# Experts of a hybrid layer: padding rows skipped in gathers and stores, results scattered to token order, plain loads at the end

## The chip, the cores and the metric

One core of a Trainium2 chip runs the whole layer in one launch. The metric is the device time of one execution in microseconds (us), lower is better. Times of several executions are given as their median.

## The reference, cut to what matters

One layer on 1024 tokens of width 1024 in float32: modulated norm, one projection, a recurrent head group and a sparse attention head group, output projection, then a mixture of experts, then a final modulated norm. The change touches the experts, their routing tables and the end.

```python
def hierarchical_moe(h, w_group, b_group, w_expert, b_expert, e_gate, e_up, e_down):
    ...
    expert = (g_sel[:, None] * EXPERTS_PER_GROUP + top_i).reshape(-1)
    token = jnp.repeat(jnp.arange(n_tok), TOP_K_EXPERT)
    ...
    def expert_block(args):
        tok, w, e = args
        xb = xf[tok]
        hid = jax.nn.silu(xb @ e_gate[e]) * (xb @ e_up[e])
        return (hid @ e_down[e]) * w[:, None].astype(xb.dtype)
    ...
    out = jnp.zeros_like(xf).at[row_tok].add(y.reshape(n_rows, D))
```

Ahead of the first lines left out a group of 8 experts is chosen for each token and the best 2 in it; then the pairs are sorted by expert, and each expert's rows are padded to whole blocks. Behind it come x = x + (1 + gate2) * moe and the final modulated norm. There are 32 experts (width 512) and 2048 pairs of a token and an expert. In blocks of 64 rows the reference's routing of its inputs needs 47 blocks: experts 0 to 7 one each, expert 8 two, 9 and 10 one each, then one or two each, never more. The pairs of experts 0 to 10 are 50, 27, 53, 17, 45, 61, 47, 40, 70, 62 and 35, in 12 blocks.

## The kernel before, in words

The program has stages, each with its own semaphores and a barrier at its end: projection, attention and recurrence, routing ("route") and experts ("experts"). Each engine's list of work is written by hand. SP issues plain DMAs on the queue q1; POOL issues DMAs on q0, among them those that are indirect, where a column of row numbers in SBUF says which rows of a DRAM tensor are moved.

**Projection.** POOL writes zeros over the whole of `expert_rows` in DRAM (L457), 34 stores of 128 rows, while TensorE projects.

**Routing.** Every pair gets a place (`dest`): its block and its row in it. VectorE builds one-hot tables of the rows and of the blocks, and multiplies the latter by the token's number (L1723 to L1726). TensorE multiplies the tables (L1782), and VectorE turns the result into the integers `idx_all` (L1728): column b holds the 64 token numbers of block b. Padding rows hold token 0.

**Experts.** A block is 64 rows. There are three slots of weights. SP fills a slot again as soon as it is free: gate and up weights of expert e+3 (L1817, L1818) after the up matmuls of expert e's last block, the down weights (L1821) after its down matmuls. Weights of experts 0 to 2 are loaded during routing. For block b:

- POOL copies the index column (L1882), waits for it and gathers the 64 token rows into one of two buffers (L1885), three blocks ahead; then it waits for the evicted result of its block and stores it (L1893).
- ScalarE takes the gathered rows (L1926), and makes the tanh of the gate (L1935).
- VectorE scales the turned rows (L1957, L1959), gates the hidden rows (L1971, L1976), and evicts the result (L1966). The result `psum["P0"]` has columns 0 to 511 of the 64 rows in partitions 0 to 63 and columns 512 to 1023 in partitions 64 to 127; it goes to `y_sb[j]`, one of two buffers. Before that VectorE waits for the store of block b-2.
- TensorE does gate (L2049), up (L2056), turning (L2062, L2035 for the next block) and down (L2073) matmuls.

The order on POOL around the store, and the pattern that takes the two halves apart:

```python
with pool.Fori(0, full) as i:
    for j in range(2):
        gather(i * 2 + j + 3, 1 - j, i * 2 + j + 2)
        store(i * 2 + j, j)
...
pool.dma_start(y_d[bass.ds(b * BLK, BLK), :].rearrange("r (h n) -> h r n", h=2), y_sb[j]).then_inc(q(f"y_stored{j}"), 16)
```

The store of the last block is issued by SP (L1853). **The end.** When all stores have landed, POOL gathers for each of eight tiles of 128 tokens the first and the second expert's row by `dest` (L1911), 16 indirect DMAs of 512 KB. SP loads the residual rows `x1` (L1856), three tiles at once after the last store, then one for each tile written. TensorE adds the two rows with their weights (L2093, weights as scaled identities of ScalarE, L1940), VectorE adds the residual (L2004), ScalarE squares (L1943), POOL takes the root (L1875), VectorE scales and shifts (L2015, L2016), SP stores the tile (L1865).

Of the kernel before, what the change touches and what calls it, by code (L numbers as in the profile page):

```python
# [20 lines left out]
I32 = mybir.dt.int32  # L21
# [38 lines left out]
ROWS = ALL_BLOCKS * BLK  # L60
# [69 lines left out]
def sparse_attention_moe_layer(nc, x, c, ada_w, ada_b, norm1_g, w_in, shift_mu, w0, w_decay_up, a0, w_aaa_up,  # L130
# [3 lines left out]
    with ExitStack() as ctx:  # L134
# [36 lines left out]
        y_d = dram("expert_rows", (ROWS, D))  # L171
# [36 lines left out]
        idx_all = sb("idx_all", [BLK, ALL_BLOCKS], I32)  # L208
# [28 lines left out]
        with ExitStack() as scope:  # L237
# [135 lines left out]
            def _(pool):  # L373
# [82 lines left out]
                for i in range(ROWS // P):  # L456
                    pool.dma_start(y_d[P * i:P * i + P, :], Z[:, :, :, :].rearrange("p a b c -> p (a b c)")).then_inc(*sig("rows_zero", i, by=16))  # L457
# [18 lines left out]
                pool.wait_ge(*at("rows_zero", ROWS // P - 1))  # L476
# [1022 lines left out]
        with ExitStack() as scope:  # L1499
# [19 lines left out]
            count_i, count_f, token_f = A.take(ALL_BLOCKS).bitcast(I32), A.take(ALL_BLOCKS), A.take(NT)  # L1519
# [86 lines left out]
            def _(dve):  # L1606
# [114 lines left out]
                dve.wait_ge(*at("tokens", 0))  # L1721
# [3 lines left out]
                by_tile = in_block.rearrange("p (t j) b -> p t j b", j=2)  # L1725
                link(dve, dve.tensor_tensor(by_tile, by_tile, token_f.unsqueeze(2).unsqueeze(3).to_broadcast([P, NT, 2, ALL_BLOCKS]), ALU.mult), "in_block", 0)  # L1726
                dve.wait_ge(*at("rows_found", 0))
                link(dve, dve.tensor_copy(idx_all[:, :], psum["W1"][0:BLK, 0:ALL_BLOCKS]), "idx_all", 0)  # L1728
# [57 lines left out]
        with ExitStack() as scope:  # L1786
# [5 lines left out]
            xT, y_sb = A.take(KD, BLK), [A.take(D // 2) for _ in range(2)]  # L1792
            hid, hidT = A.take(DE // 2), A.take(KE // 2, 2, BLK)
            index_now = [A.take(1)[0:BLK].bitcast(I32) for _ in range(2)]
# [4 lines left out]
            first, second, x1 = (A.take(NT, D) for _ in range(3))  # L1799
# [15 lines left out]
            def _(sp):  # L1815
# [35 lines left out]
                full = sp.value_load(first_block[0:1, NE + 2:NE + 3], min_val=NE // 2 - 1, max_val=MAX_BLOCKS // 2)  # L1851
# [3 lines left out]
                def load_x1(t):  # L1855
                    sp.dma_start(x1[:, t, :], x1_d[tile(t), :]).then_inc(*sig(f"x1_loaded{t}", 0, by=16))  # L1856

                sp.wait_ge(q("last_stored"), 16)
                for t in range(3):
                    load_x1(t)  # L1860
                for t in range(NT):
                    if t + 3 < NT:
                        load_x1(t + 3)
                    sp.wait_ge(*at("out", t))
                    sp.dma_start(out[0, tile(t), :], first[:, t, :]).then_inc(*sig("out_stored", t, by=16))  # L1865
# [3 lines left out]
            def _(pool):  # L1869
# [7 lines left out]
                def gather(b, j, before):  # L1877
# [7 lines left out]
                    pool.indirect_dma_start(rows_in[j], None, xn2_d[:, :], bass.IndirectOffsetOnAxis(ap=index_now[j], axis=0)).then_inc(q(f"gathered{j}"), 16)  # L1885
# [15 lines left out]
                gather(pairs * 2 + 2, 0, pairs * 2 + 1)  # L1901
                pool.wait_ge(q("gathered0"), (pairs + 2) * 16)
                pool.wait_ge(q("gathered1"), (pairs + 1) * 16)

                pool.wait_ge(q("y_stored0"), pairs * 16)
                pool.wait_ge(q("y_stored1"), full * 16)
                pool.wait_ge(q("last_stored"), 16)
                pool.sem_inc(q("stores_seen"))
# [212 lines left out]
```

## Time and profile before

| | |
|---|---|
| Median of 3 runs | 1904.99 us (1904.92 to 1906.54) |
| The profiled execution | 1907.29 us, its span 1905.3 us |
| Busy share of the span | PE 86%, DVE 47%, ACT 29%, POOL 20% |
| Mean granted clock of TensorE | 0.939 |
| q0 (DMAs of POOL) | 37200 packets, 54.08 MB, 9.0% of sixteen engines |
| q1 (DMAs of SP) | 121474 packets, 305.99 MB, 45.0% |

PE is the time of the matmuls, PEld that of loading their weights beside them; DVE is VectorE, ACT ScalarE, POOL GpSimd. The granted clock is given as a share of full speed. The span is from the first to the last instruction; the execution's own time is 2 us longer. A wait is put down to what came last. In a timeline a row such as "x32" is a group of equal instructions in a row, with the time from the first to the last. "Landing" is the time from the issue of a DMA until its data are there.

### The profile page before, as it was taken

The page shows a single profiled execution, that of the slowest core. Times are in us where ns is not written, and L with a number is a line of the kernel's source. Part 1 is how long each engine was busy: PE and PEld are TensorE (multiplying, and loading weights), DVE is VectorE, ACT ScalarE, POOL GpSimd, SP SyncE. Part 2 cuts the span into 40 slices and gives each one's busy share as a digit, 9 for nine tenths or more (in the row PEclk, how much of TensorE's full clock was granted, in tenths as well). Part 3 has the DMA queues.
Part 4 walks back from the last instruction along what each step waited for, and adds up shares of the span by engine and source line. Part 5 has one row for each costly group of instructions (what it writes and reads, how often), then busy time and mean ns, then how long its engine had stood idle before and what let it go on. Part 6 is the DMA issues. An engine that isn't in the chain of part 4 may idle for free. (4 is left out here: it accounts for less than half of the span.)

```text
span 1905.3 us, 40477 instructions
## 1 busy us (share of the span) xinstructions
PE 1645.6 (86%) x16070; PEld 1083.5 (57%) x16071; DVE 904.1 (47%) x1996; ACT 559.9 (29%) x1099; POOL 390.2 (20%) x824
## 2 busy tenths in 40 slices
PE   4999999867778889889886997588989999999966
PEld 2644444336667667667663455455556666666642
DVE  4256686257777767767652235221222222222226
ACT  4115886713334334434331111010101111011111
POOL 7601467601101110100100000111111111111113
PEclk9999999978999999999997997698999999999988
DMA  9883434320021011010002655599999999999927
GB/s 323 269 334 145 161 120 163 119 83 27 14 93 38 13 38 27 13 38 7 19 7 92 250 177 219 189 360 379 381 368 339 316 358 362 362 359 339 305 90 301
DMA packets 158802, 361.83 MB, mean 190 GB/s; under 512 B 33698, under 2 KB 71634, under 8 KB 158674
## 3 DMA queue, kind: packets, MB, share of 16 engines
q1 hardware_dynamic: 121474, 305.99, 45.0%
q0 software_dynamic: 37200, 54.08, 9.0%
q8 instruction: 87, 1.43, 0.3%
q14 instruction: 41, 0.34, 0.1%
HBM read 303.23 MB, written 56.65 MB: 189 GB/s over the span
## 5 line engine op out<-in xcount | busy, mean ns | idle before, releaser
L2049 PE MATMUL psX<-arena 128*64 128x256 f32 x1536 | 188.2, 401 | 28.1 <-DMA arena<-in_e_down_dram 26.6
L2049 PEld LDWEIGHTS psX<-arena 128*64 128x64 f32 x1536 | 119.4, 145 | 109.9 <-issue 63.0
L2073 PE MATMUL psP<-arena 128*64 128x512 f32 x768 | 175.4, 598 | 0.0
L809 PE MATMUL psX<-arena 128*128 128x512 f32 x320 | 142.6, 601 | 3.4 <-DVE arena L715 1.9
L509 ACT ACTIVATE arena<-arena 128x1024 bf16<-128x1024 f32 (+5 forms) x138 | 134.2, 973 | 32.5 <-POOL arena L466 28.6
L809 PE MATMUL psP<-arena 128*128 128x512 f32 x320 | 141.1, 595 | 2.9 <-DVE arena L715 2.9
L1893 POOL DMA_DIRECT2D expert_rows<-arena x47 | 40.9, 869 | 483.5 <-DVE arena L1966 453.3
L1740 PE MATMUL psP<-arena 128*128 128x512 f32 x256 | 117.9, 620 | 9.8 <-DVE arena L1673 4.6
L1926 ACT ACTIVATE arena<-arena 64x1024 f32<-64x1024 f32 x49 | 51.7, 1056 | 238.1 <-PE psT L2035 211.1
L1935 ACT ACTIVATE arena<-psX 128x256 f32<-128x256 f32 x48 | 18.4, 383 | 339.8 <-PE psX L2049 339.8
L1971 DVE SCALAR_TENSOR_TENSOR arena<-arena,psX 128x256 f32<-128x256 f32 x48 | 20.2, 421 | 191.4 <-ACT arena L1935 191.4
L1264 PE MATMUL psP<-ckvT,arena 128*128 128x512 f32 (+3 forms) x192 | 81.5, 537 | 33.7 <-DVE st L1103 22.5
L809 PEld LDWEIGHTS psX<-arena 128*128 128x128 f32 x320 | 60.5, 192 | 79.5 <-issue 74.0
L809 PEld LDWEIGHTS psP<-arena 128*128 128x128 f32 x320 | 59.9, 190 | 79.7 <-issue 75.4
L2073 PEld LDWEIGHTS psP<-arena 128*64 128x64 f32 x768 | 50.9, 136 | 88.0 <-issue 82.2
L2056 PE MATMUL psX<-arena 128*64 128x128 f32 x1536 | 92.1, 273 | 0.0
L2056 PE MATMUL psT<-arena 128*64 128x128 f32 x1536 | 92.1, 273 | 0.0
L1740 PEld LDWEIGHTS psP<-arena 128*128 128x128 f32 x256 | 50.1, 199 | 73.6 <-issue 72.6
L2056 PEld LDWEIGHTS psX<-arena 128*64 128x64 f32 x1536 | 87.4, 137 | 6.7
L1420 PE MATMUL psW<-arena 64*64 64x64 f32 x2304 | 78.8, 225 | 14.2 <-DVE arena L1208 14.2
L1420 PEld LDWEIGHTS psW<-arena 64*64 64x64 f32 x2304 | 73.7, 140 | 24.5 <-DVE arena L1208 18.7
L2056 PEld LDWEIGHTS psT<-arena 128*64 128x64 f32 x1536 | 85.6, 137 | 0.0
(407 smaller groups left out, 2805.3 us busy)
## 6 DMA issues: line engine op xcount, KB each, us to landing
arena<-in_e_gate_dram SPq DMA_DIRECT2D x32, 2048.0 KB, 20.1
arena<-in_e_up_dram SPq DMA_DIRECT2D x32, 2048.0 KB, 25.9
arena<-in_e_down_dram SPq DMA_DIRECT2D x32, 2048.0 KB, 27.2
arena<-in_ada_w_dram SPq DMA_DIRECT2D x12, 2048.0 KB, 14.2
expert_rows<-Z POOLq DMA_DIRECT2D x34, 512.0 KB, 16.5
expert_rows<-arena POOLq DMA_DIRECT2D x47, 256.0 KB, 14.9
proj_T<-arena SPq DMA_DIRECT2D x36, 256.0 KB, 2.0
arena<-in_x_dram SPq DMA_DIRECT2D x16, 512.0 KB, 5.7
```

The lines of the kernel that those rows point to most:

```text
L509: link(act, act.activation(junk_bf[:, 0:n], score[k][:, 0:n], ACT.Sign, scale=s_sgn[k], bias=s_neg[k], accum_out=s_sum[k]), "counted", k, i)
L809: mm = pe.matmul(psum[b], w[:, k, first:first + P], hT[:, k, 512 * half:512 * half + 512], start=(k == 0), stop=(k == KD - 1))
L1264: mm = pe.matmul(psum[f"P{half}"][:, 0:m], qlT[:, 4 * (h % 2) + h // 2, :], ckvT[:, 512 * half:512 * half + m], start=True, stop=True)
L1420: mm = pe.matmul(o, (old, new)[w], (new, old)[w], start=True, stop=True)
L1740: mm = pe.matmul(psum[f"P{half}"], kt(mixT, t)[:, k, :], wout[:, k, 512 * half:512 * half + 512], start=(k == 0), stop=(k == KD - 1))
L1893: pool.dma_start(y_d[bass.ds(b * BLK, BLK), :].rearrange("r (h n) -> h r n", h=2), y_sb[j]).then_inc(q(f"y_stored{j}"), 16)
L1926: act.activation(rows, rows_in[j], ACT.Copy).then_inc(q("rows_ready"), 1)
L1935: act.activation(hid, psum["X0"][:, 0:DE // 2], ACT.Tanh, scale=0.5).then_inc(q("tanh_done"), 1)
L1971: dve.scalar_tensor_tensor(out=hid, in0=hid, scalar=1.0, in1=psum["X0"][:, 0:DE // 2], op0=ALU.add, op1=ALU.mult).then_inc(q("half_gated"), 1)
L2049: mm = pe.matmul(psum["X0"][BLK * h:BLK * h + BLK, 0:DE // 2], xT[:, k, :], gate_w[u][:, k, DE // 2 * h:DE // 2 * (h + 1)], start=(k == 0) ...
L2056: mm = pe.matmul(psum[("X1", "T1")[f]][BLK * h:BLK * h + BLK, 0:P], xT[:, k, :], up_w[u][:, k, at_col:at_col + P], start=(k == 0), stop=(k ...
L2073: mm = pe.matmul(psum["P0"][BLK * half:BLK * half + BLK, :], hidT[:, f, h, :], down_w[u][:, KE // 2 * h + f, D // 2 * half:D // 2 * (half ...
```

## The change

Numbers of pairs, 2 x token + j, take the place of token numbers: `expert_rows` has 2048 rows, two for each token, in token order. Padding rows get the number 4096. From the table `pair_all` come the token numbers (`idx_all`, half of it: 2048 for padding, outside of the 1024 rows). Gathers and stores are indirect with a bounds check, and rows out of bounds are left out. In blocks 0 and 1 padding is clamped to row 1023, so that both buffers hold numbers. The result is evicted in two halves so that each of 64 partitions holds a whole row, and POOL scatters it. The second buffer of results is `Z`. The zeros of the projection stage are gone. At the end SP loads the residual rows once expert 29 is done (in slot 2, which is then free), and after the last scatter the pairs of rows of each tile with one plain load of 1 MB.

```diff
-ROWS = ALL_BLOCKS * BLK
+NO_PAIR = 4 * SEQ
...
-        y_d = dram("expert_rows", (ROWS, D))
+        y_d = dram("expert_rows", (2 * SEQ, D))
...
-                for i in range(ROWS // P):
-                    pool.dma_start(y_d[P * i:P * i + P, :], Z[:, :, :, :].rearrange("p a b c -> p (a b c)")).then_inc(*sig("rows_zero", i, by=16))
...
+                for j in range(2):
+                    link(pool, pool.tensor_scalar(pair_f[:, :, j], token_f, 2.0, float(j - NO_PAIR), ALU.mult, ALU.add), "pairs", j)
...
-                link(dve, dve.tensor_copy(idx_all[:, :], psum["W1"][0:BLK, 0:ALL_BLOCKS]), "idx_all", 0)
+                step(dve.tensor_scalar(pair_all[:, :], psum["W1"][0:BLK, 0:ALL_BLOCKS], float(NO_PAIR), None, ALU.add))
+                step(dve.tensor_scalar(idx_all[:, :], pair_all[:, :], 1, None, ALU.logical_shift_right))
+                link(dve, dve.tensor_scalar(idx_all[:, 0:2], idx_all[:, 0:2], SEQ - 1, None, ALU.min), "idx_all", 0)
...
-                sp.wait_ge(q("y_ready"), pairs * 2 + 1)
-                sp.dma_start(y_d[bass.ds((full * 2 + 1) * BLK, BLK), :].rearrange("r (h n) -> h r n", h=2), y_sb[1]).then_inc(q("last_stored"), 16)
...
+                sp.wait_ge(q("y_done"), two_left + 1)
+                for t in range(NT):
                     sp.dma_start(x1[:, t, :], x1_d[tile(t), :]).then_inc(*sig(f"x1_loaded{t}", 0, by=16))
...
+                for j in range(2):
+                    sp.wait_ge(q(f"y_stored{j}"), pairs * 16)
+                for t in range(NT):
+                    sp.dma_start(both[:, t], y_d[2 * P * t:2 * P * t + 2 * P, :].rearrange("(p j) n -> p j n", j=2)).then_inc(*sig(f"y_loaded{t}", 0, by=16))
...
-                    pool.indirect_dma_start(rows_in[j], None, xn2_d[:, :], bass.IndirectOffsetOnAxis(ap=index_now[j], axis=0)).then_inc(q(f"gathered{j}"), 16)
+                    pool.indirect_dma_start(rows_in[j], None, xn2_d[:, :], bass.IndirectOffsetOnAxis(ap=index_now[j], axis=0),
+                                            bounds_check=SEQ - 1, oob_is_err=False).then_inc(q(f"gathered{j}"), 16)
...
-                    pool.dma_start(y_d[bass.ds(b * BLK, BLK), :].rearrange("r (h n) -> h r n", h=2), y_sb[j]).then_inc(q(f"y_stored{j}"), 16)
+                    pool.sem_inc(q("y_seen"))
+                    pool.tensor_copy(place_now[j], pair_all[:, bass.ds(b, 1)]).then_inc(q("place_ready"), 1)
+                    pool.wait_ge(q("place_ready"), b + 1)
+                    pool.sem_inc(q("place_seen"))
+                    pool.indirect_dma_start(y_d[:, :], bass.IndirectOffsetOnAxis(ap=place_now[j], axis=0), y_sb[j], None,
+                                            bounds_check=2 * SEQ - 1, oob_is_err=False).then_inc(q(f"y_stored{j}"), 16)
...
-                    dve.tensor_tensor(y_sb[j], psum["P0"], gate_half, ALU.mult).then_inc(q("y_ready"), 1)
+                    dve.tensor_tensor(y_sb[j][:, 0:D // 2], psum["P0"][0:BLK], gate_half[0:BLK], ALU.mult).then_inc(q("y_half"), 1)
+                    dve.wait_ge(q("y_half"), b + 1)
+                    dve.tensor_tensor(y_sb[j][:, D // 2:D], psum["P0"][BLK:P], gate_half[BLK:P], ALU.mult).then_inc(q("y_ready"), 1)
```

POOL's list of work at the end of the loop over blocks and after it, before (a name such as `expert_rows<-arena 2x64x512` is destination, source and shape; 48 blocks, the last without a store on POOL):

```order
L1893 DMA expert_rows<-arena 2x64x512
L1882 ISA
L1882 COPY arena<-idx_all 64x1
L1883 REGISTER_ALU
L1885 DMA arena<-xn_rows,arena 64x1024
L1902 ISA
L1903 ISA
L1905 REGISTER_ALU
L1906 REGISTER_ALU
L1911 DMA arena<-expert_rows,dest 128x1024 x10
```

and now:

```order
L1894 DMA expert_rows<-arena 2048x1024
L1878 ISA
L1878 COPY arena<-idx_all 64x1
L1879 REGISTER_ALU
L1881 DMA arena<-xn_rows,arena 64x1024
L1889 REGISTER_ALU
L1891 ISA
L1891 COPY arena<-pair_all 64x1
L1894 DMA expert_rows<-Z,arena 2048x1024
L1905 ISA
L1906 ISA
L1871 TENSOR_TENSOR st<-st,mhalf 128x1 x8
```

The gathers at the end have left POOL, the last store has come to it, and each store has a copy of its row numbers ahead.

SP's list of work after the last weights, before:

```order
L1853 DMA expert_rows<-arena 2x64x512
L1856 DMA arena<-x_rows 128x1024 x4
L1865 DMA out_dram<-arena 128x1024
L1856 DMA arena<-x_rows 128x1024
L1865 DMA out_dram<-arena 128x1024
```

and now:

```order
L1852 REGISTER_ALU
L1854 DMA arena<-x_rows 128x1024 x8
L1856 REGISTER_ALU
L1858 DMA arena<-expert_rows 128x2048 x8
L1861 DMA out_dram<-arena 128x1024 x8
```

All loads of residual rows stand ahead of the wait for the stores, and the result's loads follow it.

## Rows read from the trace of the kernel before

**Rows 1.** Busy time: length, PE, PEld, DVE, ACT, POOL, clock, DMA share, GB/s.
```profile
1216.00:1415.00 199.00, 173.24 (x1588) 115.96 (x1590) 45.46 (x103) 18.70 (x26) 25.01 (x37) 0.92 0.99 356
1415.00:1841.00 426.00, 425.20 (x4270) 288.36 (x4266) 124.00 (x280) 49.32 (x69) 70.08 (x105) 1.00 0.94 322
```

**Rows 2.** Waits of TensorE, 1206 to 1842 us: total, times, longest.
```profile
PE psX L2049 <- DMA arena<-in_e_down_dram: 26.6, 7, 7.6
```

**Rows 3.** Timeline of TensorE, gate matmuls: start, length, engine, line, [idle before <-releaser].
```profile
1215.90 5.98 PE L2049 MATMUL psX<-arena 128*64 128x256 f32 x32 [1.51 <-DVE arena L1959]
...
1270.88 5.36 PE L2049 MATMUL psX<-arena 128*64 128x256 f32 x32 [3.87 <-DMA arena<-in_e_down_dram]
...
1414.81 3.62 PE L2049 MATMUL psX<-arena 128*64 128x256 f32 x32
```

**Rows 4.** Chain that ended last, 1236 to 1410 us: start, length, what.
```profile
1242.76 27.78 DMA arena<-in_e_down_dram
...
1368.49 31.55 DMA arena<-in_e_down_dram
```

**Rows 5.** DMA, 1206 to 1242 us, in 40 slices.
```profile
GB/s 405 423 414 405 164 196 59 189 335 223 350 378 182 96 232 41 0 0 0 0 0 0 14 114 337 396 400 423 405 419 405 419 428 373 406 379 383 388 401 383
```

**Rows 6.** DMA, 1842 to 1851 us: busy tenths and GB/s in 40 slices.
```profile
DMA  0000000111111201101111111111111111100000
GB/s 0 0 0 0 0 0 0 36 18 18 46 27 55 18 0 55 18 27 46 46 46 46 55 55 46 55 46 55 55 46 55 46 55 55 46 0 0 0 0 0
```

**Rows 7.** Timeline in the middle of the experts; landings of L1885 (gather) and L1893 (store).
```profile
1512.32 0.69 DVE L1966 TENSOR_TENSOR arena<-psP,ckvT 128x512 f32<-128x512 f32 x1 [2.07 <-PE psP L2073]
...
1514.55 0.20 POOL L1882 COPY arena<-idx_all 64x1 int32 x1
...
1515.57 0.93 POOL L1885 DMA_INDIRECT arena<-xn_rows,arena  x1 [0.81 <-POOL arena L1882]
...
1516.10 0.42 DVE L1971 SCALAR_TENSOR_TENSOR arena<-arena,psX 128x256 f32<-128x256 f32 x1 [3.09 <-ACT arena L1935]
...
1520.52 1.06 ACT L1926 ACTIVATE arena<-arena 64x1024 f32<-64x1024 f32 x1 [4.46 <-PE psT L2035]
...
1524.47 0.69 DVE L1966 TENSOR_TENSOR arena<-psP,ckvT 128x512 f32<-128x512 f32 x1 [2.07 <-PE psP L2073]
...
DMA to landing us min/median/max: 4.3/15.2/16.2
...
DMA to landing us min/median/max: 9.2/14.9/15.8
```

**Rows 8.** Timeline and chain of the tail; landing of L1856 (residual rows, plain load).
```profile
1841.40 0.69 DVE L1966 TENSOR_TENSOR arena<-psP,ckvT 128x512 f32<-128x512 f32 x1 [2.07 <-PE psP L2073]
...
1842.30 7.94 DMA expert_rows<-arena
...
1851.05 7.68 DMA arena<-expert_rows,dest
...
1858.87 5.38 PE L2093 MATMUL psP<-arena 128*128 128x512 f32 x8 [17.61 <-DMA arena<-expert_rows,dest]
...
1871.81 1.22 DVE L2004 TENSOR_TENSOR arena<-psX,arena 128x1024 f32<-128x1024 f32 x1
...
1879.94 1.23 DVE L2004 TENSOR_TENSOR arena<-psP,arena 128x1024 f32<-128x1024 f32 x1
...
1886.00 1.23 DVE L2004 TENSOR_TENSOR arena<-psT,arena 128x1024 f32<-128x1024 f32 x1 [2.08 <-DMA arena<-x_rows]
...
DMA to landing us min/median/max: 3.2/7.5/9.8
```

**Rows 9.** Timeline of VectorE, end of routing.
```profile
1193.70 0.18 DVE L1718 TENSOR_SCALAR arena<-dest 128x16 int32<-128x16 int32 x1
...
1202.25 0.22 DVE L1728 CAST idx_all<-psW 64x68 int32<-64x68 f32 x1 [4.05 <-PE psW L1782]
```

**Rows 10.** Busy time, 80 to 140 us (columns as in rows 1).
```profile
80.00:140.00 60.00, 57.90 (x215) 25.99 (x214) 32.61 (x79) 9.73 (x19) 18.76 (x35) 1.00 0.85 332
```

More of the change, by code:

```diff
@@ L1720, in _ @@
                 step(dve.tensor_copy(place_f[1], place_i[1]))
-                dve.wait_ge(*at("tokens", 0))
+                dve.wait_ge(*at("pairs", 1))
                 dve.wait_ge(*at("out_done", NT - 1))
@@ L1791, in sparse_attention_moe_layer @@
             rows_in, rows = [piece[0:BLK] for piece in pieces], pieces[0][BLK:P]
-            xT, y_sb = A.take(KD, BLK), [A.take(D // 2) for _ in range(2)]
+            xT, y_sb = A.take(KD, BLK), [A.take(D)[0:BLK], Z[0:BLK].rearrange("p a b c -> p (a b c)")]
             hid, hidT = A.take(DE // 2), A.take(KE // 2, 2, BLK)
-            index_now = [A.take(1)[0:BLK].bitcast(I32) for _ in range(2)]
+            index_now, place_now = ([A.take(1)[0:BLK].bitcast(I32) for _ in range(2)] for _ in range(2))
             assert A.at <= WEIGHTS_AT
@@ L1798, in sparse_attention_moe_layer @@
             A.at = 0
-            first, second, x1 = (A.take(NT, D) for _ in range(3))
+            both, x1 = A.take(NT, 2, D), A.take(NT, D)
             assert A.at == (SLOTS - 1) * (2 * KD * DE + KE * D)
@@ L1901, in _ @@
                 gather(pairs * 2 + 2, 0, pairs * 2 + 1)
+                store(full * 2 + 1, 1)
                 pool.wait_ge(q("gathered0"), (pairs + 2) * 16)
                 pool.wait_ge(q("gathered1"), (pairs + 1) * 16)
[L1905 to L1908, printed above, removed]
                 for t in range(NT):
-                    for j, dst in enumerate((first, second)):
-                        pool.indirect_dma_start(dst[:, t, :], None, y_d[:, :], bass.IndirectOffsetOnAxis(ap=dest[:, t, j:j + 1], axis=0))\
-                            .then_inc(*sig(f"gathered{j}{t}", 0, by=16))
-                    if t >= 4:
-                        roots(t - 4)
-                for t in range(NT - 4, NT):
                     roots(t)
@@ L2014, in write @@
                         dve.wait_ge(*at("rows_loaded", 3))
-                    step(dve.scalar_tensor_tensor(out=first[:, t, :], in0=res[:, b, :], scalar=s_x[:, 16 + t:17 + t], in1=gain_row, op0=ALU.mult, op1=ALU.mult))
-                    link(dve, dve.tensor_tensor(first[:, t, :], first[:, t, :], shift_row, ALU.add), "out", t)
+                    step(dve.scalar_tensor_tensor(out=both[:, t, 0, :], in0=res[:, b, :], scalar=s_x[:, 16 + t:17 + t], in1=gain_row, op0=ALU.mult, op1=ALU.mult))
+                    link(dve, dve.tensor_tensor(both[:, t, 0, :], both[:, t, 0, :], shift_row, ALU.add), "out", t)
                 add(0)
@@ L2087, in _ @@
                         pe.wait_ge(*at("x2", t - 4))
-                    for j, rows_of in enumerate((first, second)):
+                    pe.wait_ge(*at(f"y_loaded{t}", 0))
+                    for j in range(2):
                         pe.wait_ge(*at("weights", t, j))
-                        pe.wait_ge(*at(f"gathered{j}{t}", 0))
                         for half in range(2):
                             part = slice(512 * half, 512 * half + 512)
-                            mm = pe.matmul(psum["PTXW"[t % 4] + str(half)], weigh[:, t, j, :], rows_of[:, t, part], start=(j == 0), stop=(j == 1))
+                            mm = pe.matmul(psum["PTXW"[t % 4] + str(half)], weigh[:, t, j, :], both[:, t, j, part], start=(j == 0), stop=(j == 1))
                     mm.then_inc(*sig("combined", t))
```

18 lines of the change are left out of this document (5 added, 13 removed).

## The prediction

> **What bounds the kernel now.** I read the page's engine shares, then busy time by stretch, then the waits of TensorE, then single timelines. The experts take the last third. From 1216 to 1415 us TensorE is busy 173 of 199 us at a mean granted clock of 0.92; from 1415 to 1841 it is busy 425 of 426 us at 1.00 [rows 1]. So the first stretch can be shortened from outside and the second cannot. The waits of TensorE name the landing of the down weights, 26.6 us over seven times [rows 2]. After a wait the gate matmuls also run long: 5.36 us for 32 instead of 3.62 [rows 3]. Undisturbed, one block follows another after 12.15 us (1512.32 to 1524.47, two evictions in [rows 7]). The first block starts at 1215.90 and the fourteenth at 1414.81 [rows 3]; thirteen blocks at 12.15 are 157.9 us, so 41.0 us are lost. The first block's slow start is 2.4 of it (5.98 against 3.62). **38.6 us** hang on the weights, and a single 0.8 us wait later on.
>
> The weights come in 2.097 MB transfers. Where they flow freely, in seven slices in a row, the sixteen DMA engines move 400 to 428 GB/s [rows 5], about 412, or 5.1 us a transfer. The down weights of expert 4 land at 1270.5 and those of expert 11 at 1400.0 [rows 4]: 129.5 us for 21 transfers, which alone need 107.1. The other 22.4 us fall on the eight blocks computed between them, **2.8 us for each pair** of a gather and a store. By their bytes (0.524 MB) they should cost 1.27. The remaining 1.53 us is the shape of the store, I think. The last store of the kernel runs with nothing beside it, and it moves at 46 to 55 GB/s, with the engines busy at one tenth [rows 6]: two engines out of sixteen. Its shape is halves, rows, columns, 2x64x512, like all the other stores. Weights striped over all engines must wait for the two that are late.
>
> The tail is a serial chain: eviction to 1842.1, store to 1850.2, gather to 1858.7, the first combining matmuls (5.4 us), then VectorE at 4.07 us a tile to the end (1871.81 to 1879.94 are two), with one wait of 2.08 us for residual rows [rows 8].
>
> **The change, part by part.**
>
> *Zero stores (34 of 512 KB) removed.* They lie in 80 to 140 us, where TensorE is busy 57.9 of 60 us [rows 10], and nothing there waits for a DMA. At most the 2.1 us of idle time comes back; I take 0. Their cover is the projection's matmuls.
>
> *Two tables instead of one.* The conversion of 0.22 us becomes one of the same size plus two integer operations on the path to the first gather, of some 0.18 us as their neighbour [rows 9]: **+0.4 us**. The two POOL operations that number the pairs stand far ahead of a wait.
>
> *Eviction in two halves.* 64x512 twice instead of 128x512 once: 0.69 us again if time goes by the columns, 0 if by bytes; I take 0.7. In the loop this is free: VectorE's next work is 3.8 us after the eviction's start (1512.32 to 1516.10, [rows 7]) and the two halves end after 1.4.
>
> *Scatter instead of store.* POOL gains a copy and the wait for it, 1.02 us by the gather's (1514.55 to 1515.57, [rows 7]). Queued behind it is the next gather. It is now issued 0.7 + 1.0 us later. Today it is issued at 1515.57 and lands 15.2 us later, at 1530.8. ScalarE takes a block's rows every 12.15 us; the row at 1520.52 is the block before, so these rows are taken at 1532.7. The slack of 1.9 us shrinks to 0.2, and the rows so taken are turned by TensorE only some ten microseconds later (in its next block). Free.
>
> *Less and better spread traffic.* The reference's routing gives 47 blocks and an empty one. The first twelve blocks hold 507 pairs in 768 rows. The stores move 507 rows, the gathers 558, since the first two blocks clamp their padding to a real row. That is 0.69 of the bytes, 0.88 us a pair of transfers. With 64 rows as the leading dimension the scatter has the shape of the gather. For the cost of its shape the bounds are 0 and the 1.53 us of today; I take 0.2, near the lower end, since a 64-row gather shows no two-engine pattern. A pair then costs 1.1 us and **saves 1.7** (bounds 0.4 and 1.9). Twelve pairs lie before expert 11's weights, whose landing ends the last large wait: **-20.4 us**, and the late 0.8 us wait goes too: -21.2.
> The Trainium skill (DMA: Bandwidth & Descriptors, "Why a DMA increments its semaphore by 16 and not by 1") says that a transfer is split over the largest number of engines up to sixteen that divides both sides' slowest dimension; this gives two engines for today's store and sixteen for the scatter. By this rule, the trace agrees on the two.
>
> *Tail.* The last eviction ends 0.7 us later, 1842.8. POOL: 0.68 to react, 1.02 for the copy and its wait, issue at 1844.5. Landing: a gather of 64 rows takes at least 4.3 us [rows 7]; 1848.8. A plain load of 512 KB takes at least 3.2 us [rows 8]; 1 MB adds 1.3, so the first tile is there at 1853.4 against 1858.7: **-5.3 us**. After that a tile's load takes 2.6 us (1.049 MB at 412 GB/s) and VectorE needs 4.07, so VectorE remains the bound; residual rows loaded since expert 29 is done (over three blocks, 36 us, ahead of the end) take away the **2.0 us** wait (1879.94 to 1886.00 is 6.06). Tail: -7.3.
>
> **Sum:** 0 + 0.4 - 21.2 - 7.3 = -28.1 us. The profiled execution took 1907.29 us with a span of 1905.3; it becomes 1879.2. The median of the runs lies 2.3 us under that execution, so I forecast **1877 us**.
>
> **Rivals.**
>
> *A. Only bytes count.* If the two-engine store costs nothing of itself, and the 1.53 us are general loss between competing queues, a pair saves only 0.4 us: 12 x 0.4 = 4.8, and 7.3 in the tail, less 0.4: 1905.0 - 11.7 = 1893. For it: engines show busy all the time in the saturated stretch. Against it: the 46 GB/s. Chance 0.20. The Trainium skill (DMA: Bandwidth & Descriptors, "Where 436 GB/s comes from") puts the limit of HBM at about 358 GB/s for one core, under which spreading gives nothing and only bytes count, this case. By this rule, the trace disagrees: 400 to 428 GB/s in the slices of [rows 5].
>
> *B. The stream falls in step with TensorE.* Fewer delays compound, no weights are late, and all 39.4 us come back: 1905.0 - 39.4 - 7.3 + 0.4 = 1859. Against it: weights at 5.1 us a transfer and 1.1 a pair make 16.4 us an expert, while one-block experts take 12.15, and eight of these come first. Chance 0.07.
>
> *C. The scatter is slow, and the kernel slower.* The eviction of block b waits for the store of b-2. The scatter is issued at 1512.32 + 1.4 + 0.68 + 1.02 = 1515.4, the next eviction from that buffer starts at 1536.6, and VectorE has 2.4 us to spare behind it: landings up to 23.6 us are free (now 14.9, [rows 7]). Each microsecond more costs one per two blocks, 18 in the stretch that TensorE bounds. From 25.2 us on (18 x 1.56 = 28.1) the kernel is no faster than before; at 26 us it takes 1877 + 43 = 1920. For it: row writes to scattered places of memory, bounds to be checked on each row. Against it: gathers of 64 rows issued behind a store land in 15.2. Chance 0.05.
>
> *D. Rows out of bounds are moved all the same*, so that only the shape changes: a pair saves 2.8 - 1.27 - 0.2 = 1.33, twelve 16.0; 1905.0 - 16.8 - 7.3 + 0.4 = 1881. Chance 0.08, inside my range.
>
> The forecast keeps 0.60. The range goes from 1864, halfway to B, to 1895, past A; outside lie most of B and C, and some error of the terms. A measurement of this kernel can tell about 0.2%, 4 us, from no change. Faster by more than that: all but C and a mishap in the terms, 0.92; within it 0.03; slower 0.05.
>
> **What would show it.** In the new profile TensorE's waits for the down weights should fall from 26.6 to about 12 us and the fourteenth block start 20 us earlier; the down weights of experts 4 and 11 should land some 116 us apart (107.1 and 8 x 1.1) or less. From there to the last eviction the time should not change. The scatter should land well under 15 us. In the tail the first combining matmul should start about 10.7 us after the last eviction ends (16.8 now), with no wait for residual rows. I am wrong on the shape if a pair still costs over 2 us; on the tail if the scatter takes over 8 us alone, like the last store now; and C holds if evictions wait for the scatter.

## The result, and the profile after

| | before | changed |
|---|---|---|
| Median of the runs | 1904.95 us (1901.53 to 1906.54, 4 runs) | 1873.31 us (1869.89 to 1879.42, 4 runs) |
| The profiled execution, its span | 1907.29 us, 1905.3 us | 1870.82 us, 1869.1 us |
| q0 (DMAs of POOL) | 37200 packets, 54.08 MB | 9024 packets, 19.00 MB |

The ratio is 0.9836, 95% interval 0.9817 to 0.9855: 31 us faster. The forecast was 1877 us.

Busy time of the changed kernel by stretch (columns as in [rows 1]), from the first gate matmul to that of the fourteenth block, and on to the last eviction; and TensorE's wait for the down weights between 1190 and 1842 us:

```profile
1209.00:1386.00 177.00, 164.35 (x1586) 111.36 (x1586) 53.65 (x115) 18.70 (x26) 28.21 (x49) 0.96 0.98 381
1386.00:1813.00 427.00, 425.41 (x4272) 288.64 (x4268) 149.34 (x317) 49.27 (x70) 79.37 (x140) 1.00 0.85 319
```

```profile
PE psX L2043 <- DMA arena<-in_e_down_dram: 12.6, 4, 4.8
```

The first stretch is 22 us shorter, the second as long as before within 1 us, and as full. The waits for the down weights have fallen from 26.6 us in seven to 12.6 in four [rows 2]. The timeline of the gate matmuls (columns as in [rows 3]) and the chain of waits (start, length, what) show where weights are still late:

```profile
1208.78 5.23 PE L2043 MATMUL psX<-arena 128*64 128x256 f32 x32 [1.51 <-DVE arena L1951]
...
1258.98 3.62 PE L2043 MATMUL psX<-arena 128*64 128x256 f32 x32
1273.04 3.67 PE L2043 MATMUL psX<-arena 128*64 128x256 f32 x32 [1.74 <-DMA arena<-in_e_down_dram]
1290.19 5.36 PE L2043 MATMUL psX<-arena 128*64 128x256 f32 x32 [4.79 <-DMA arena<-in_e_down_dram]
1305.98 3.67 PE L2043 MATMUL psX<-arena 128*64 128x256 f32 x32 [1.73 <-DMA arena<-in_e_down_dram]
1322.74 6.26 PE L2043 MATMUL psX<-arena 128*64 128x256 f32 x32 [4.39 <-DMA arena<-in_e_down_dram]
...
1386.11 3.62 PE L2043 MATMUL psX<-arena 128*64 128x256 f32 x32
```

```profile
1247.04 25.66 DMA arena<-in_e_down_dram
...
1297.05 25.35 DMA arena<-in_e_down_dram
```

The first gate matmuls are slow as before (5.23 us; 5.98 before, and 5.0 to 6.0 over all profiles of this document). The four blocks behind the first then start without a wait, and the fourteenth starts 177.3 us after the first, not 198.9. Of the 41.0 us lost over thirteen blocks 19.4 are left. The down weights of expert 5 land at 1272.70 and those of expert 8 at 1322.40: 49.7 us for nine transfers and three pairs. At the 5.1 us a transfer that the prediction used, a pair costs 1.3 us. But the loads of the changed kernel run at 419 GB/s, not 411 (shown below), which is 5.0 us a transfer, and by that a pair costs 1.5 us (both are estimates).

The steady state of the changed kernel (timeline, then the times from issue to landing of the gathers, L1881, minimum/median/maximum):

```profile
1483.59 0.68 DVE L1958 TENSOR_TENSOR arena<-psP,ckvT 64x512 f32<-64x512 f32 x1 [2.06 <-PE psP L2067]
1484.31 0.69 DVE L1960 TENSOR_TENSOR arena<-psP,ckvT 64x512 f32<-64x512 f32 x1
1485.24 0.18 POOL L1891 COPY arena<-pair_all 64x1 int32 x1 [8.15 <-DVE arena L1960]
1486.30 0.93 POOL L1894 DMA_INDIRECT expert_rows<-arena  x1 [0.88 <-POOL arena L1891]
...
1487.23 0.20 POOL L1878 COPY arena<-idx_all 64x1 int32 x1
1487.37 0.42 DVE L1965 SCALAR_TENSOR_TENSOR arena<-arena,psX 128x256 f32<-128x256 f32 x1 [2.37 <-ACT arena L1927]
1488.27 0.96 POOL L1881 DMA_INDIRECT arena<-xn_rows,arena  x1 [0.85 <-POOL arena L1878]
...
DMA to landing us min/median/max: 2.0/6.3/7.5
```

VectorE's next work comes 3.8 us after the eviction's start, as before [rows 7]. Gathers land in 6.3 us where it was 15.2 (medians), and the completion events of the scatters come 2.0 to 7.2 us after their issue, where a store took 9.2 to 15.8.

The tail of the changed kernel, from its timeline and its chain:

```profile
1811.55 0.68 DVE L1958 TENSOR_TENSOR Z<-psP,ckvT 64x512 f32<-64x512 f32 x1 [2.07 <-PE psP L2067]
1812.27 0.69 DVE L1960 TENSOR_TENSOR Z<-psP,ckvT 64x512 f32<-64x512 f32 x1
...
1813.20 0.18 POOL L1891 COPY arena<-pair_all 64x1 int32 x1 [8.16 <-DVE Z L1960]
```

```profile
1814.26 2.01 DMA expert_rows<-Z,arena
...
1816.34 4.96 DMA arena<-expert_rows
```

```profile
1821.39 6.14 PE L2087 MATMUL psP<-arena 128*128 128x512 f32 x8 [9.98 <-DMA arena<-expert_rows]
...
1827.57 1.23 DVE L1998 TENSOR_TENSOR arena<-psP,arena 128x1024 f32<-128x1024 f32 x1 [14.60 <-PE psP L2087]
...
1831.06 1.23 DVE L1998 TENSOR_TENSOR arena<-psT,arena 128x1024 f32<-128x1024 f32 x1 [0.76 <-PE psT L2087]
...
1835.08 1.23 DVE L1998 TENSOR_TENSOR arena<-psX,arena 128x1024 f32<-128x1024 f32 x1
```

The last eviction ends at 1812.96, the scatter takes 2.01 us, the first tile 4.96, and the first combining matmul starts 8.4 us after the eviction's end (16.8 before, [rows 8]). From then to the end of the span it takes 47.7 us, where it took 46.4, although the wait for residual rows is gone. The records of the barrier's line, with their lengths in ns (minimum/median/maximum), and the waits of SP's queue behind 1855 us (total, times, longest) tell why; first two rows before, then three of the changed kernel:

```profile
L1786 POOLq DRAIN  x1: 3373/3373/3373, 1898.1 to 1898.1; - x1
...
SPq L1786 <- PEq L1786: 0.2, 1, 0.2
```

```profile
L1786 POOLq DRAIN  x1: 8759/8759/8759, 1859.3 to 1859.3; - x1
...
SPq L1786 <- PEq L1786: 2.9, 1, 2.9
SPq L1786 <- DMA out_dram<-arena: 2.2, 1, 2.2
```

The drain with which POOL closes the stage lasts 8.76 us where it lasted 3.37. It starts behind the last root, at 1859.25, and ends at 1868.01, 2.9 us after the last output has landed; SP, and with it the end of the kernel, wait for it.

### The profile page after: what moved, and what is told of

Read it like the earlier page. It is cut to its first block and busy times, and to the rows that moved or that the text cites. A ratio compares the mean times of both kernels' runs of the same rounds, so it can differ in the third digit from the quotient of the medians.

```text
span 1869.1 us, 40718 instructions
## 1 busy us (share of the span) xinstructions
PE 1629.8 (87%) x16070; PEld 1075.9 (58%) x16071; DVE 937.1 (50%) x2046; ACT 559.8 (30%) x1099; POOL 369.4 (20%) x825
## 3 DMA queue, kind: packets, MB, share of 16 engines
q0 software_dynamic: 9024, 19.00, 3.5%
## 5 line engine op out<-in xcount | busy, mean ns | idle before, releaser
L2043 PE MATMUL psX<-arena 128*64 128x256 f32 x1536 | 180.0, 388 | 14.2 <-DMA arena<-in_e_down_dram 12.6
L2043 PEld LDWEIGHTS psX<-arena 128*64 128x64 f32 x1536 | 115.2, 140 | 91.4 <-issue 43.5
L2050 PEld LDWEIGHTS psX<-arena 128*64 128x64 f32 x1536 | 87.4, 137 | 6.7
L1891 POOL COPY arena<-pair_all 64x1 int32 x48 | 8.5, 177 | 414.7 <-DVE arena L1960 215.0
L1417 PEld LDWEIGHTS psW<-arena 64*64 64x64 f32 x2304 | 75.1, 142 | 24.5 <-DVE arena L1205 19.4
L462 POOL TENSOR_SCALAR arena<-arena 128x1 f32<-128x1 f32 x132 | 58.0, 440 | 146.9 <-ACT arena L506 139.9
## 6 DMA issues: line engine op xcount, KB each, us to landing
arena<-in_e_up_dram SPq DMA_DIRECT2D x32, 2048.0 KB, 15.2
```

The costliest lines, as they stand in the source:

```text
L462: step(pool.tensor_scalar(s_hit[k], s_sum[k], s_lim[k], s_step[k][:, i - 1:i], ALU.is_gt, ALU.mult))
L1417: mm = pe.matmul(o, (old, new)[w], (new, old)[w], start=True, stop=True)
L2043: mm = pe.matmul(psum["X0"][BLK * h:BLK * h + BLK, 0:DE // 2], xT[:, k, :], gate_w[u][:, k, DE // 2 * h:DE // 2 * (h + 1)], start=(k == 0) ...
L2050: mm = pe.matmul(psum[("X1", "T1")[f]][BLK * h:BLK * h + BLK, 0:P], xT[:, k, :], up_w[u][:, k, at_col:at_col + P], start=(k == 0), stop=(k ...
```

## The experiments

Each ratio is to the kernel before, timed beside that version on the same chip (its medians there are 1903.4 to 1907.7 us; the first row is the one beside the changed kernel's first runs). The stretches come from one profile of each version. "Experts" is the time from the first gate matmul to that of the fourteenth block in the profiled execution, "tail" that from the last eviction's end to the first combining matmul, then from there to the end of the span.

| Version | Median, us | Ratio, 95% interval | Before the experts | Experts | Tail |
|---|---|---|---|---|---|
| before | 1904.95 | | 1215.9 | 198.9 | 16.8 + 46.4 |
| changed | 1873.31 | 0.9836 (0.9817 to 0.9855) | 1208.8 | 177.3 | 8.4 + 47.7 |
| changed, again | 1873.16 | 0.9821 (0.9804 to 0.9838) | 1211.2 | 177.5 | 8.3 + 47.7 |
| changed, a third time | 1872.28 | 0.9832 (0.9815 to 0.9848) | 1209.3 | 178.9 | 8.3 + 47.2 |
| zero stores back | 1872.75 | 0.9831 (0.9812 to 0.9849) | 1207.3 | 177.9 | 8.1 + 47.0 |
| before, store of 64x4 KB | 1892.49 | 0.9925 (0.9910 to 0.9941) | 1212.8 | 188.8 | 12.0 + 50.3 |
| before, two stores of 64x2 KB | 1887.89 | 0.9907 (0.9885 to 0.9930) | 1216.9 | 187.6 | 12.5 + 46.9 |
| changed, padding moved | 1881.99 | 0.9870 (0.9849 to 0.9890) | 1210.8 | 185.1 | 9.3 + 47.4 |
| the same, padding reads spread | 1880.39 | 0.9870 (0.9851 to 0.9890) | 1210.2 | 184.0 | 9.5 + 47.5 |
| the same, gathers as before | 1882.82 | 0.9868 (0.9852 to 0.9885) | 1213.2 | 184.4 | 9.8 + 47.0 |
| the same, plain store | 1882.45 | 0.9887 (0.9869 to 0.9905) | 1205.4 | 184.6 | 8.5 + 47.9 |
| changed, residual rows late | 1874.64 | 0.9832 (0.9813 to 0.9852) | 1213.1 | 176.9 | 9.3 + 47.3 |
| changed, early drain | 1869.57 | 0.9817 (0.9798 to 0.9835) | 1212.4 | 178.0 | 8.1 + 44.7 |
| changed, early drain, again | 1869.77 | 0.9819 (0.9800 to 0.9837) | 1211.1 | 178.2 | 8.2 + 44.8 |

From the fourteenth block's gate matmul to that of the last block all versions took 413.0 us (413.1 with two stores), the kernel before 414.1.

**The changed kernel again.**

> The changed kernel as it is, on the chip of the next three, as their measure. First block of the experts (first gate matmul) near 1209 us as in its first profile if the 7 us won ahead of the experts belong to the change, anywhere between 1209 and 1216 if they are the scatter of single executions. Time near 1873 us.

It repeats: the experts' stretch and the tail agree within 0.2 us, the time ahead of the experts varies by 2.4. In the third profile the experts took 178.9 us, so this stretch varies by 1.6 us from one profile to the next.

**Zero stores back.** 34 stores of zeros, as before, but to a tensor of their own:

```diff
+zero_d = dram("zero_rows", (ALL_BLOCKS * BLK, D))
+for i in range(ALL_BLOCKS * BLK // P):
+    pool.dma_start(zero_d[P * i:P * i + P, :], Z[...]).then_inc(*sig("rows_zero", i, by=16))
+pool.wait_ge(*at("rows_zero", ALL_BLOCKS * BLK // P - 1))
```

> The changed kernel with the 34 zero stores of the projection stage put back (into a tensor that nothing reads). If they were free, as predicted: the same time within 2 us, and the first gate matmul of the experts where it is without them. If the 7 us ahead of the experts come from their removal: 5 to 8 us slower, all of it before the experts.

Nothing moved: 0.9831 against 0.9821 and 0.9832. Their removal is worth nothing that can be measured.

**The shape of the store alone.** The kernel before, with the eviction in halves and a store whose leading dimension is the 64 rows:

```diff
-pool.dma_start(y_d[bass.ds(b * BLK, BLK), :].rearrange("r (h n) -> h r n", h=2), y_sb[j])
+pool.dma_start(y_d[bass.ds(b * BLK, BLK), :], y_sb[j])
 ...
-dve.tensor_tensor(y_sb[j], psum["P0"], gate_half, ALU.mult)
+dve.tensor_tensor(y_sb[j][:, 0:D // 2], psum["P0"][0:BLK], gate_half[0:BLK], ALU.mult)
+dve.tensor_tensor(y_sb[j][:, D // 2:D], psum["P0"][BLK:P], gate_half[BLK:P], ALU.mult)
```

> The kernel before with one part of the change: the result is evicted in two halves so that a store is 64 rows of 4 KB instead of 2x64x512; all else (padding, zeros, gathers at the end) as before. Shape theory: 1.3 to 1.5 us less for each pair of a gather and a store, 16 to 18 us until the fourteenth block, and some 4 us in the tail since the last store lands in about 4 us instead of 7.9: 1883 to 1886 us. Bytes theory (rival A): nothing in the experts, at most the tail's 4 us: 1901 us.

The experts took 188.8 us, 10.1 less than before; TensorE's waits for the down weights sum to 18.8 us in five. The time, 1892.5 us, lies between the two theories (1883 to 1886 and 1901), and neither was right on its size.

**Padding moved.** The changed kernel, but every padding row of a block gets a valid place: the gather reads row 1023 for it, the scatter writes it to a spare row of its own behind the 2048:

```diff
-step(dve.tensor_scalar(pair_all[:, :], psum["W1"][...], float(NO_PAIR), None, ALU.add))
+step(dve.scalar_tensor_tensor(out=pair_all[:, :], in0=psum["W1"][...], scalar=float(NO_PAIR), in1=spare[0:BLK], op0=ALU.add, op1=ALU.min))
-link(dve, dve.tensor_scalar(idx_all[:, 0:2], idx_all[:, 0:2], SEQ - 1, None, ALU.min), "idx_all", 0)
+link(dve, dve.tensor_scalar(idx_all[:, :], idx_all[:, :], SEQ - 1, None, ALU.min), "idx_all", 0)
 ...
-    bounds_check=2 * SEQ - 1
+    bounds_check=2 * SEQ + ALL_BLOCKS * BLK - 1
```

> The changed kernel, but padding rows are moved too: gathered from row 1023, scattered to rows of their own that nothing reads. Shape theory: the bytes are worth 0.4 us a pair, so about 5 us slower than the changed kernel (1878 us). Bytes theory: they are all of the gain in the experts, so 20 us slower (1893 us or more).

185.1 us: 7.8 more than the changed kernel, 3.7 less than the version with the new shape alone, though both move the same rows. The padding is worth more than I gave it, the shape less, and something between these two versions has a price of its own. Of the next four runs three look for it in the padding's reads, the form of the store and the form of the gather; the other asks what the shape itself is worth.

**Padding reads spread.**

```diff
-link(dve, dve.tensor_scalar(idx_all[:, :], idx_all[:, :], SEQ - 1, None, ALU.min), "idx_all", 0)
+link(dve, dve.tensor_scalar(idx_all[:, :], idx_all[:, :], SEQ - 1, None, ALU.bitwise_and), "idx_all", 0)
```

> The run in which padding rows are moved as well (1881.99 us), with one difference: its padding gathers all read row 1023, here each reads a row of its own (the index's low ten bits). Theory 1, what the padding costs is its bytes and their packets: the same as that run within 1.5 us, some 8 us over the changed kernel, the experts (first gate matmul to that of the fourteenth block) again 185 us. Theory 2, part of it is the reading of one row by all of a block's rows at once: up to 3 us faster than that run, the experts 182 to 183 us, and then the bytes are worth what the prediction gave them (4.7 us).

184.0 us and the same ratio: that the padding of a gather reads one and the same row costs about 1 us at most, no more than one profile differs from the next. What the padding costs is its traffic.

**Two stores of 64x2 KB.**

```diff
-pool.dma_start(y_d[bass.ds(b * BLK, BLK), :].rearrange("r (h n) -> h r n", h=2), y_sb[j])
+for h in range(2):
+    pool.dma_start(y_d[bass.ds(b * BLK, BLK), D // 2 * h:D // 2 * h + D // 2], y_sb[j][BLK * h:BLK * h + BLK])
```

> The kernel before with its one store of a block's rows (128 pieces of 2 KB from all partitions, which the trace shows on two of the 16 DMA engines) split in two stores of 64 x 2 KB each, without the change of the eviction, without scatter, with all padding. Theory, the price of the old store was its being on two engines: as the run with the 64 x 4 KB store (1892.5 us, the experts 188.8 us long against 198.9), so 1890 to 1894 us and landings of 4 to 7 us in place of 15; the second store adds one issue of about 1 us to POOL, which has room. Rival, the gain of that run came from the eviction in halves or the row of 4 KB: no gain, about 1903 us. If this form is itself on few engines, its landings stay at 15 us and the time at 1900 or over, and the run says nothing on the rival.

187.6 us: as the version with 4 KB rows, so the eviction in halves and the row length are not the cause. The stores' completion events come 5.3 to 5.4 us after the issue (medians of the two buffers; 14.9 in the kernel before), as they should if two stores of 64 rows are spread and one of 2x64x512 is not. Spreading the store is what pays, 10 to 11 us in the experts.

**A plain store.** The kernel with padding moved, with the rows stored in block order to the spare rows, and these combined in the tail, so the results do not reach their tokens:

```diff
-pool.tensor_copy(place_now[j], pair_all[:, bass.ds(b, 1)])
-pool.indirect_dma_start(y_d[:, :], bass.IndirectOffsetOnAxis(ap=place_now[j], axis=0), y_sb[j], None, ...)
+pool.dma_start(y_d[bass.ds(b * BLK + 2 * SEQ, BLK), :], y_sb[j])
```

> The run with all padding rows moved (experts 185.1 us from first gate matmul to that of the fourteenth block, 1881.99 us), but a block's rows go out by one plain store of 64 x 4 KB to the spare rows in block order, in place of the scatter; the tail reads those spare rows, so the results are not put in token order: same bytes, same loads. It asks where the 3.7 us lie between the version of the kernel before with the 64 x 4 KB store (188.8 us) and that run. Theory 1, a plain store of these rows costs the weights more than a scatter of them: experts 188 to 189 us. Theory 2, the form of the store is worth nothing, the difference is in the gathers (padding reads row 1023 in place of row 0) or in the zero stores' being gone: experts 184.5 to 185.5 us. By the closing drain (10.0 us in the version with the 64 x 4 KB plain store, 3.7 with two plain stores of 2 KB rows, 8.8 with scatters) it should be 9 to 10 us here.

184.6 us: a scatter costs the weights' stream no more and no less than a plain store of the same rows. The closing drain lasted 8.76 us, as with scatters, not 10.

**Gathers as before.**

```diff
-link(dve, dve.tensor_scalar(idx_all[:, :], idx_all[:, :], SEQ - 1, None, ALU.min), "idx_all", 0)
+link(dve, dve.scalar_tensor_tensor(out=idx_all[:, :], in0=idx_all[:, :], scalar=float(SEQ), in1=idx_all[:, :], op0=ALU.is_lt, op1=ALU.mult), "idx_all", 0)
 ...
-pool.indirect_dma_start(rows_in[j], None, xn2_d[:, :], ..., bounds_check=SEQ - 1, oob_is_err=False)
+pool.indirect_dma_start(rows_in[j], None, xn2_d[:, :], ...)
```

> The run with all padding rows moved (experts 185.1 us, 184.6 with a plain store), with its gathers put back to the form of the kernel before: padding reads row 0 in place of row 1023, and the gather has no bound. Theory 1, the 4 us between that run and the kernel before with the 64 x 4 KB store (188.8 us) lie in the gathers: experts 188 to 189 us, some 3 to 4 us over the 1881 to 1882 of the runs with padding. Theory 2, the gathers' form is worth nothing, and the 4 us are in what else separates the two (the zero stores' being gone, the order in which SP reaches its loads, where rows lie in memory): experts 184.5 to 185.5 us, the time unchanged.

184.4 us: nothing in the gathers either. What differs between the versions is the rate of all loads. The DMA view from 1300 to 1370 us (GB/s in 40 slices, then the sum) of the version with the 64x4 KB store, and of the one with padding moved:

```profile
GB/s 407 426 300 351 412 412 412 410 410 410 410 412 255 377 407 410 403 412 410 412 412 407 257 379 410 412 412 407 412 407 412 384 267 403 410 410 410 410 382 267
DMA packets 6984, 27.17 MB, mean 388 GB/s; under 512 B 352, under 2 KB 352, under 8 KB 6984
```

```profile
GB/s 421 365 358 426 419 421 419 426 419 421 300 417 421 426 417 421 428 417 410 414 410 267 377 407 412 417 426 424 419 304 360 389 379 393 393 407 286 419 419 417
DMA packets 7141, 27.81 MB, mean 397 GB/s; under 512 B 352, under 2 KB 352, under 8 KB 7141
```

The undisturbed slices stand at 410 to 412 in the first and at 417 to 428 in the second. The same split is there from 9 to 25 us, when all versions load the same first inputs and no row of an expert exists; the sums of that window, of the kernel before and then of the changed one:

```profile
DMA packets 1722, 6.58 MB, mean 411 GB/s; under 512 B 105, under 2 KB 118, under 8 KB 1722
```

```profile
DMA packets 1898, 6.70 MB, mean 419 GB/s; under 512 B 170, under 2 KB 292, under 8 KB 1898
```

In this window the three versions of the kernel before all move 411 GB/s, the eleven profiles of the changed one and its versions 417 to 420. It is not the mix of packets: in the records of single packets the same ones of 4096 bytes take 162.6 or 162.7 ns on average in the three, and 159.0 to 159.6 in the eleven. Nor is it the size of `expert_rows`, which is 4352 rows in the three and 2048 or 6400 in the eleven. A difference between the two groups that nothing in the experiments undid is where the arena begins, into which these inputs and the expert weights are loaded: 61,664 bytes into each partition before, 32 over a multiple of 64, and 61,952 with the new table `pair_all` ahead of it, a multiple of 64. A run that shifts the arena alone by 32 bytes was not made, so this cause is argued, not shown; and that the 3.7 us in the experts come from the rate is an estimate that fits (it is worked out below), with no run that has the one without the other.

**Residual rows late.**

```diff
-sp.wait_ge(q("y_done"), two_left + 1)
-for t in range(NT):
-    sp.dma_start(x1[:, t, :], x1_d[tile(t), :]).then_inc(*sig(f"x1_loaded{t}", 0, by=16))
 ...
 for t in range(NT):
+    sp.dma_start(x1[:, t, :], x1_d[tile(t), :]).then_inc(*sig(f"x1_loaded{t}", 0, by=16))
     sp.dma_start(both[:, t], y_d...)
```

> The changed kernel with the early load of the residual rows undone: each tile's residual row block (0.5 MB) is issued just ahead of the two expert rows of that tile (1 MB), after the last scatter has landed. Theory, the residual rows are worth something only through the bytes that now stand ahead of a tile: first tile complete after 1.5 MB in place of 1 MB, which at the 4.96 us that the first 1 MB takes to land is up to 2.5 us later, and the following tiles of 1.5 MB per some 3.6 us keep up with the 4.03 us that VectorE takes for a tile: 1.5 to 3 us slower than the changed kernel (about 1875.5). Rival, that the early loads cost the last expert blocks as much as they save (4 MB out of the weights' stream while experts still wait for it): equal to the changed kernel, with the stretch of the last 34 blocks (413.0 us) shorter by 1 to 2 us.

The first combining matmul came 9.3 us after the eviction, 0.9 to 1.0 later than in the changed kernel; the tiles then kept VectorE's 4.03 us, with no wait for residual rows (the seven steps from tile to tile take 27.64 us, 27.65 in the changed kernel). So the wait of 2.08 us before did not need the early load to go. In both versions no load stands behind a written tile any more, as it did before; that this removed the wait is argued. The whole time shows no difference that can be measured. The early load is worth 1 us by the profile, less than expected, and takes nothing from the experts (413.0 us in both), so the rival fell.

**Early drain.** The changed kernel, with one drain of POOL in its idle time behind the last scatter:

```diff
 pool.wait_ge(q("gathered1"), (pairs + 1) * 16)
+pool.sem_inc(q("tail_seen"))
+pool.drain()
 for t in range(NT):
     roots(t)
```

> The changed kernel with one added instruction: GpSimd drains right behind its last scatter of expert rows, where it then stands idle for some 15 us, ahead of the eight roots. In the changed kernel the drain that closes the last stage lasts 8.8 us behind the last root (8.7 to 8.8 in three runs with this tail, 10.0 in the version whose expert rows go out by a plain store, 3.4 in the kernel before) and ends 2.9 us after the last output has landed. Theory 1, the drain clears what the transfers of the expert loop left in the queue, once: the added drain takes some 8 us under cover, the closing one is down to about 3.4 us or less, the wait of 2.9 us is gone and the time is 2.5 to 3 us below the changed kernel's (about 1870.5 against 1873.2). Theory 2, the drain has a length of its own behind an expert loop, whatever ran ahead of it: both last 8 to 9 us and nothing changes (within 1 us). Theory 3, its length comes from the eight powers just ahead of it: the added one is short, the closing one still 8.8, and nothing changes.

The records of the added line and of the barrier's line:

```profile
L1908 POOLq DRAIN  x1: 9067/9067/9067, 1818.5 to 1818.5; - x1
...
L1786 POOLq DRAIN  x1: 651/651/651, 1863.0 to 1863.0; - x1
```

The added drain takes 9.07 us while POOL would wait anyway, the closing one 0.65, of which 0.55 is the last root. The stretch from the first combining matmul to the end is 44.7 us, 3.0 less, as theory 1 had it. Once more, beside the changed kernel:

> The changed kernel once more, on the same chip as the next run, which in the last call was not timed beside it: 0.982 of the kernel before, its closing drain again 8.8 us.

> The version with GpSimd's drain moved ahead of the roots once more, beside the changed kernel. In its first profile the added drain took 9.07 us (1818.55 to 1827.62, under the wait for the first combined tile), the closing one 0.65 us, and the stretch from the first combining matmul to the end was 44.7 us against 47.7. Theory, those 3 us are whole-time microseconds: median 2 to 4 us below the changed kernel of this call. Rival, something behind the profiled part takes them back: within 1 us of it.

44.8 us against 47.2, and medians of 1869.77 and 1872.28 us. The ratios to before, 0.9819 and 0.9832, have overlapping intervals, so the 2.5 us rest on the profiles: each of the two has the stage 2.4 to 3.0 us shorter. This is the fastest version measured.

## Why the prediction was right, and where it was not

The forecast of 1877 us lies 3.7 us over the measured 1873.3. The profiled execution was forecast to fall by 28.1 us; it fell by 36.5, the medians by 31.6. 7.1 us of the profiles' difference lie ahead of the experts. The mechanism was right (a store on few engines and rows of padding delay the weights, and the tail is a serial chain), but the sizes of its parts were not, and they partly cancelled.

- **Zero stores, 0:** right, by the run that brought them back.
- **Eviction in halves:** right. The two take 0.68 and 0.69 us, and in the loop they are free.
- **Experts, -20.4 and -0.8:** -21.6 and -1.1. The sum held. Its parts over the twelve pairs did not:

| Part of the experts' stretch | Forecast, us | Measured, us | From |
|---|---|---|---|
| shape of the store | 16.0 (12 x 1.33) | 10.1 and 11.3 | the kernel before with either spread store |
| padding rows | 4.7 (12 x 0.39) | 6.7 | 184.5 (mean of the four that move padding) - 177.8 (mean of the seven that do not) |
| rate of all loads | none | 3.7 | 188.2 (mean of the two spread stores) - 184.5 |

The step that failed is "The remaining 1.53 us is the shape of the store", of which 1.33 a pair was taken back: the runs show about 0.9 a pair. The padding was priced too low, at the rate of free loads. The third part came out of the weights' own 5.1 us a transfer, which the prediction held fixed: 1.9% more rate (419 against 411) over 185 us is an estimated 3.5 us. That the total came out is therefore partly luck. Together they are 21.1 of the 21.6 us. The sign "a pair still costs over 2 us" did not come up although the term was off by a third: at 1.3 or 1.5 us a pair stays under it.

- **Ahead of the experts, +0.4:** the two added operations lie where they were expected and take 0.42 us (the table is ready at 1195.81 us, the conversion ends at 1195.39). But the three profiles of before's family reach the experts at 1212.8 to 1216.9 us, the eleven others at 1205.4 to 1213.2, means 1215.2 and 1210.3. The faster loads would act here as well, but profiles scatter by 4 us (1207.3 to 1211.2 for the changed one and that with zeros back, whose times agree), so I leave it open.
- **Tail, -5.3 for the first tile:** -7.7 (8.4 in place of 16.8, and the eviction 0.7 longer). The term that was mis-sized is the scatter's landing, 4.3 us; it was 2.01. From the eviction's end to the issue it took 1.3 us, not 1.7. The DMA view of the changed kernel, 1812 to 1820 us, shows why:

```profile
DMA packets 182, 0.84 MB, mean 104 GB/s; under 512 B 80, under 2 KB 80, under 8 KB 80
...
q0 software_dynamic: 80, 0.00, 0.4%
```

The last block is the empty one: its scatter is 80 small packets with no data to speak of, and moves no row. Where the padding is moved, the last scatter lands in 3.25 us and the two ends are 9.3 us apart. The loads of 1 MB I had at 4.5 us; 4.96.
- **Residual rows, -2.0:** the wait is gone, and the seven steps of VectorE from tile to tile take 27.65 us where they took 29.77. But it also goes when these rows are loaded late, so the reason the prediction gave, the early load, is not what took it away; the early load itself is worth 1 us, at the first tile. And 1.3 us net were lost again, which the prediction had nowhere: 2.7 at the drain (2.9 us of waiting in place of 0.2), 0.8 at the first combining matmuls (6.14 us, 5.38 before), less the 2.1. Net tail -6.4, forecast -7.3.

**The rivals.** A (only bytes count) fell by the two runs on the shape, which move the same bytes and gain 10.1 and 11.3 us. The limit of about 358 GB/s for one core that the Trainium skill gives (DMA: Bandwidth & Descriptors, "Where 436 GB/s comes from") is passed in every undisturbed slice, at 410 to 428. B: the stream still loses 19.4 us, so it did not fall in step. C: scatters land in 7.2 us at most, and no eviction waits for one. D: rows out of bounds are not moved: over the experts' first stretch q0 carries 4.64 MB in the changed kernel and 6.82 in the version that moves the padding. D's price of 1881 us is near that version's 1881.99, though its parts were others.

The check by the landing of the down weights of expert 11 could not be made: nothing waits for them any more, and the profile of the changed kernel has no landing for them.

## What to carry to other kernels

When weights stream from memory on all DMA engines, look at every small transfer beside them for its spread: a store of 2x64x512 that runs on two engines cost the stream more than its bytes, and the last transfer of the kernel, which runs alone, shows that rate undisguised. Price a gain in a shared stream by undoing each part on its own, since a sum can be right with its parts wrong, as here. And when a tail shrinks, follow every engine to the barrier: here POOL's own closing drain took back 2.7 us, and one drain in its idle time returned them.

## What the runs showed of the hardware

- A drain of POOL has a length that is not that of the work just ahead of it: 8.76 us in the changed kernel and its versions without the early drain (the one with a plain store too), 3.37 in the kernel before, 3.71 with two stores of 64x2 KB, 9.99 with one of 64x4 KB, each time behind the same root of 0.55 us. A second drain, 35 us after the first and with no DMA of POOL between them, took 0.65 us. So something that stood ahead of the first drain is cleared once, and eight roots do not bring it back. That the DMAs of POOL leave it is likely, since with all else as in the kernel before the form of the stores changes the length (3.37, 3.71, 9.99), but not shown; what sets the length stays open.
- The rate of all plain loads differed by 2% between two families of programs (411 and 417 to 420 GB/s from 9 to 25 us; undisturbed slices at 410 to 412 and at 417 to 428 in the expert loop) that run the same loads there. The cause is open.
- Rows left out by the bounds of an indirect DMA still send small packets: from 1300 to 1370 us the changed kernel has 520 packets under 512 bytes, the version that moves the padding 352. They cost less than the rows: the last scatter lands in 2.01 us with all of its rows left out, in 3.25 with all moved.
- The number of packets fell most by the shape: from 1300 to 1370 us the kernel before has 2106 packets under 512 bytes, the one with the 64x4 KB store 352 and the one with two stores of 64x2 KB 416.
